# Two-layer hybrid network on one core: the first mixer's order of chunks, delta rule and closing products

## The reference, cut to what matters

```python
def token_mixer(h, w_in, w_out, ...):
    qkv_a, a_a, b_a, z_a, qkv_b, qk_c, v_c, i_c, f_c, o_c = split(h @ w_in)
    qa, ka, va = split(causal_conv_silu(qkv_a, gdn_conv), 3)     # 4 taps, 6 heads of 64
    qa, ka = l2norm(qa), l2norm(ka)
    g = -exp(gdn_a_log) * softplus(a_a + gdn_dt_bias); beta = sigmoid(b_a)
    oa = gated_delta_rule(qa, ka, va, g, beta)   # inverts (I + A), A strictly lower, by blocks
    oa = oa * rsqrt(mean(oa * oa) + eps) * gdn_norm * silu(z_a)
    ob = moba_attention(*split(qkv_b, 3))        # 4 heads, causal here
    qc, kc = split(causal_conv_silu(qk_c, mlstm_conv), 2)
    hc = mlstm_chunkwise(qc, kc, v_c, i_c + i_bias, log_sigmoid(f_c + f_bias))
    hc = hc * sigmoid(o_c); hc = layer_norm_per_head(hc) * mlstm_norm
    return concatenate([oa, ob, hc]) @ w_out
```

## Time and profile before

| | |
|---|---|
| median of 3 runs | 2487.0 us |
| profiled execution | 2486.44 us |
| its span | 2484.6 us |
| mean granted TensorE clock | 0.918 |
| TensorE busy | 2158.2 us (87%) |
| VectorE busy | 1630.8 us (66%) |
| ScalarE busy | 1096.3 us (44%) |
| first mixer stage, first input tile to next stage | 279.4 to 577.4 us |
| second mixer stage | 991.3 to 1289.8 us |

### The profile page before, as it was taken

How to read it: one execution, slowest core, us unless ns; L and a number is a source line. 1 busy time by engine, 2 the same in 40 slices (tenths; PEclk the granted TensorE clock), 3 DMA queues, 4 the chain that set the end, 5 groups by cost and what they waited for, 6 DMA issues and landing times. The chain is left out here.

```text
span 2484.6 us, 35604 instructions
## 1 busy us (share of the span) xinstructions
PE 2158.2 (87%) x14856; PEld 1991.6 (80%) x14856; DVE 1630.8 (66%) x2221; ACT 1096.3 (44%) x1535; POOL 332.8 (13%) x281
## 2 busy tenths in 40 slices
PE   6999887988998999878979986977799979677998
PEld 6998777877997997778969965965699769556996
DVE  6877756448777766664476644874588548746884
ACT  3443452334434444523344433553456346534552
POOL 0000302112001000222030002430110014203000
PEclk9999888988999999889989997987899989887999
DMA  9878431125786665321135642421145534112443
GB/s 379 315 282 314 162 126 60 52 85 203 281 308 238 244 254 212 145 86 60 69 111 221 223 184 93 164 85 52 68 170 187 203 121 153 68 68 72 177 178 117
DMA packets 59792, 409.13 MB, mean 165 GB/s; under 512 B 6832, under 2 KB 7088, under 8 KB 12912
## 3 DMA queue, kind: packets, MB, share of 16 engines
q1 hardware_dynamic: 53424, 384.00, 41.4%
q0 software_dynamic: 5920, 22.43, 2.4%
q10 hardware_dynamic: 288, 0.42, 0.0%
HBM read 403.68 MB, written 3.15 MB: 164 GB/s over the span
## 5 line engine op out<-in xcount | busy, mean ns | idle before, releaser
L573 DVE TENSOR_TENSOR l<-w,h 128x2048 fp32r<-128x2048 f32 x296 | 687.9, 2327 | 251.7 <-ACT h L558 236.2
L674 PE MATMUL ps<-xh,h 128*128 128x256 f32 x2672 | 780.3, 292 | 61.2 <-DVE l L573 29.2
L675 PE MATMUL ps<-xl,h 128*128 128x256 f32 x2672 | 766.7, 287 | 0.0
L676 PE MATMUL ps<-xh,l 128*128 128x256 f32 x2672 | 765.4, 286 | 0.0
L558 ACT CAST h<-w 128x2048 fp32r<-128x2048 f32 x296 | 557.2, 1887 | 314.7 <-PE ps L704 170.7
L674 PEld LDWEIGHTS ps<-xh,h 128*128 128x128 f32 x2672 | 524.4, 196 | 79.9 <-DVE l L573 30.0
L675 PEld LDWEIGHTS ps<-xl,h 128*128 128x128 f32 x2672 | 523.8, 196 | 1.9 <-issue 1.9
L676 PEld LDWEIGHTS ps<-xh,l 128*128 128x128 f32 x2672 | 523.0, 196 | 0.0
L702 PE MATMUL ps<-h,hh 128*128 128x512 f32 x528 | 207.8, 394 | 0.0
L703 PE MATMUL ps<-l,hh 128*128 128x512 f32 x528 | 205.8, 390 | 0.0
L704 PE MATMUL ps<-h,hl 128*128 128x512 f32 x528 | 205.8, 390 | 0.0
(11 more groups left out here) (412 smaller groups left out, 3130.0 us busy)
## 6 DMA issues: line engine op xcount, KB each, us to landing
w<-in_stream SPq DMA_DIRECT2D x362, 1024.0 KB, 4.8
GB<-in_vec POOLq DMA_DIRECT2D x20, 512.0 KB, 6.2
gate<-in_vec POOLq DMA_DIRECT2D x6, 512.0 KB, 4.0
w<-in_stream SPq DMA_DIRECT2D x4, 512.0 KB, 3.7
cst<-in_cst POOLq DMA_DIRECT2D x1, 1160.0 KB, 13.8
memf<-in_memT SPq DMA_DIRECT2D x1, 1024.0 KB, 8.6
xf<-in_xT POOLq DMA_DIRECT2D x1, 1024.0 KB, 10.2
kv<-mk POOLq DMA_DIRECT2D x2, 512.0 KB, 6.9
```

The lines of the kernel that those rows point to most:

```text
L573: e.tensor_tensor(k.L[m % NH][:, 0:z], k.W[n % NW][:, 0:z], k.H[m % NH][:, 0:z], SUB).then_inc(k.lo_done, 1)
L674: p.matmul(P[:, 0:T], H[:, r, o], xh[:, r, :], start=r == 0, stop=False)
L675: p.matmul(P[:, 0:T], H[:, r, o], xl[:, r, :], start=False, stop=False)
L676: i = p.matmul(P[:, 0:T], L[:, r, o], xh[:, r, :], start=False, stop=r == 7)
```

## The change

The 24 gate columns become one chunk of 128 columns in four groups of 6 with 26 zero columns behind each, so that one feature tile has the gates on partitions 0, 32, 64 and 96: `gt`, its copies and its transposes go. The rows' arithmetic reads that tile's bank, which is free again once ScalarE's exponential has read it. The chunks come in another order, `AFTER` is written anew, the delta rule starts with the decays, takes logarithms three together and exponentials three together, uses banks 2, 3, 4, 5 up to the end of the levels, and lets the Q products alternate with the turns; U and V of a level stand behind different tiles. Bank 3 gets a handshake with the adaptive matmuls. The SiLU calls move. The output chunks come in reverse, so that the delta rule's features are needed last, and its last steps stand between and behind output chunks.

```diff
-    tm = [r(1152, 1164) + r(3468, 3480)]
+    row = lambda *at: sum([r(a, a + 6) + [None] * 26 for a in at], [])
+    tm = [row(1152, 3474, 1158, 3468)]
...
-MIX1 = [0, 1, 2, 3, 8, 9, 10, 14, 4, 5, 6, 7, 15, 16, 11, 12, 13]
+MIX1 = [0, 1, 9, 2, 10, 3, 14, 8, 6, 15, 7, 16, 5, 11, 4, 12, 13]
-WOUT1 = [0, 1, 2, 3]
+WOUT1 = [3, 2, 1, 0]
...
 def pe_ada(k, p, m):
+        if 3 in k.freed:
+            p.wait_ge(*k.freed.pop(3))
...
+        k.freed[3] = (k.ada_fin, FIN[v, h] + 1)
...
-GBANK = bank_table((2, 4, 5), nm=3, dk=6, be=2, A=6, Q=6, U0=4, ...)
+GBANK = bank_table((2, 3, 4, 5), dk=6, nm=3, be=2, A=6, Q1=2, U0a=2, Q2=2, U0b=2, Q3=2, ...)
...
+GBANK.update(bank_table((4, 5), u1=1, r2=1, u2=1, o=2, mx=3))
...
-AFTER = ["", "r", "r", "r", "r", "r", "r", "r", "rg", "gg", "gg", "gg", "gg", "gg", "ggb", "ggb", "ggb", "ggb", "ggb", "ggb", "ggb", "ggb", "ggb", "gg", "ggm",
-         "ggm", "ggm", "ggm", "ggm", "gm", "gm", "g", "gmg"]
+AFTER = ["r", "r", "r", "r", "rr", "r", "r", "g", "g", "gg", "", "gg", "g", "gb", "ggb", "ggb", "ggb", "ggb", "ggb", "ggb", "ggb", "ggb",
+         "ggm", "ggm", "ggm", "ggm", "ggm", "ggm", "ggm", "gggm", "gm", "gm"]
...
-    out += [(x,) for x in "gmgmgbm"] + [("out", 0), ("m",), ("m",), ("out", 1)]
+    out += [(x,) for x in "gbmgmgm"] + [("out", 0), ("g",), ("out", 1), ("g",), ("g",)]
...
 def pe_rows(k, p, l):
-    P = take(k, p, 4)
-    p.wait_ge(k.m1_gate, 8 * l + 8)
-    for a in range(2):
-        i = p.transpose(P[:, a * 128:a * 128 + 128], k.gt[:, a, :], k.ident)
...
 def dve_rows(k, v, l):
+    t = TILE[FIRST["win", l, 0]]
+    P, hb = k.ps[t % 2], k.HD[:, 2 * l:2 * l + 1]
     v.wait_ge(*k.rg(l, "zero", 2))
-    v.wait_ge(*k.rp(l, "tr"))
+    v.wait_ge(k.tile_pe, t + 1)
...
 def pe_gdn(k, p, l):
+    yield from pe_decays(...)
     yield
     for i in range(3):        # sums of squares
...
-    yield from pe_decays(...)
...
+    score(0); yield; turn(0); yield; score(1); yield; turn(1); yield; score(2); yield
+    for lv in range(1, 7):    # levels, U0 now being turn()
...
-    p.wait_ge(k.m1_silu, 5 * l + 3)
+    p.wait_ge(k.m1_silu, 5 * l + 5)
...
 def act_gdn(k, e, l):
+    yield from act_decays(...)
     e.wait_ge(*k.lg(STAGES.index(("mix1", l, 0)) - 1, "x", 3))
...
         e.activation(x, rr(bank("nm", i)[:, :], ...), ACT.Ln, bias=1e-6)
-        e.wait_ge(*ga(l, "nm", 2 * i))
+        if i < 2:
+            yield
+    for i in range(3):
+        e.wait_ge(*ga(l, "nm", i))
         e.activation(x, x, ACT.Exp, scale=-0.5)
...
 def act_mix1(k, e, s, feed):
-        if (n, j) == (8, 0):
+        if (n, j) == (3, 1):
             silu(k.gq[:, 0:3, :], 5)
             silu(k.gq[:, 3:6, :], 5)
-        if (n, j) == (15, 0):
-            silu(k.gq[:, 6:9, :], 13)
-            silu(k.cq[:, 0:3, :], 13)
-            silu(k.cq[:, 3:6, :], 13)
+        if (n, j) == (5, 1):
+            silu(k.cq[:, 0:3, :], 9)
+            silu(k.cq[:, 3:6, :], 9)
+        if (n, j) == (12, 0):
+            silu(k.gq[:, 6:9, :], 7)
+        if (n, j) == (12, 1):
+            e.activation(k.zs[:, :, :], k.zs[:, :, :], ACT.Silu)
         if (n, j) == (13, 1):
-            e.activation(k.zs[:, :, :], k.zs[:, :, :], ACT.Silu)
             e.activation(k.so[:, :, :], k.so[:, :, :], ACT.Sigmoid)
...
 def pool_mix1(k, g, s):
-    pool_rms(k, g, l, k.gv, k.gg, ...)
     pool_rms(k, g, l, k.mv_, k.mg, ...)
+    pool_rms(k, g, l, k.gv, k.gg, ...)
```

More of the change, by code:

```diff
@@ L142, in pack @@
         elif k == "win":
-            w = km(inp["w_in"][c[1]][:, MIXCOLS[c[2]][1]])
+            cols = MIXCOLS[c[2]][1]
+            w = np.zeros((D, len(cols)), np.float32)
+            at = [i for i, x in enumerate(cols) if x is not None]
+            w[:, at] = inp["w_in"][c[1]][:, [cols[i] for i in at]]
+            w = km(w)
         elif k == "wout":
@@ L235 @@
     FIRST.setdefault(_c, _n)
-CONVS = [g for n in MIX1 if MIXCOLS[n][0] == "fm" for g in ((2 * n - 2, 2 * n - 1) if n < 10 else (18,)) if g < 15]
+CONVS = [g for n in MIX1 if n and MIXCOLS[n][0] == "fm" for g in ((2 * n - 2, 2 * n - 1) if n < 10 else (18,)) if g < 15]
 def chunk_of(s):
@@ L248, in n_tiles @@
         return 0
-    return 1 if c[0] == "win" and c[2] == 10 else 2
+    return 1 if c[0] == "win" and c[2] in (0, 10) else 2
 TILE = [0]
@@ L1604, in pe_gdn, with score, turn @@
     p.wait_ge(*gv(l, "kb", 2))
[L1605 to L1612, removed]
+    for g in range(6):
+        b = GBANK["A", g]
+        pe_units(k, p, kk, k.kb, g, take(k, p, b)).then_inc(s, 1)
+        k.freed[b] = gv(l, "A", g)
+        if g % 2:
+            yield
+    def score(n):
+        for g in (2 * n, 2 * n + 1):
+            b = GBANK["Q", g]
+            pe_units(k, p, kk, q, g, take(k, p, b)).then_inc(s, 1)
+            k.freed[b] = gv(l, f"Q{n}", g % 2)
+    def turn(n):
+        for g in (2 * n, 2 * n + 1):
+            b = GBANK["U0", g]
+            P = take(k, p, b)
+            p.wait_ge(*gg(l, "part0", g))
+            for j in range(3):
+                i = p.matmul(P[:, j * 128:j * 128 + 128], k.Al[:, 3 * g + j, :], k.ident, start=True, stop=True)
+            i.then_inc(s, 1)
+            k.freed[b] = X0(2 * g)
+    X0 = lambda i: gv(l, "X0" + "ab"[i // 4], i % 4)
+    score(0)
+    yield
+    turn(0)
+    yield
+    score(1)
+    yield
+    turn(1)
+    yield
+    score(2)
+    yield
+    for lv in range(1, 7):
         for g in range(4):
@@ L1699, in dve_gdn @@
     bank = lambda name, i: k.ps[GBANK[name, i]]
+    v.wait_ge(*k.lg(STAGES.index(("mix1", l, 0)) - 1, "x", 3))
+    yield from dve_decays(k, v, l, 0, lambda g: GBANK["dk", g], gp, gv, k.Dk)
     yield
-    for i in range(3):
-        v.wait_ge(*ga(l, "nm", 2 * i + 1))
-        for j in (2 * i, 2 * i + 1):
-            v.scalar_tensor_tensor(out=gq[:, j, :], in0=gq[:, j, :], scalar=0.125 if j < 3 else 1.0, in1=k.rs[:, j, :], op0=MUL, op1=MUL).then_inc(s, 1)
-        yield
-    yield from dve_decays(k, v, l, 0, lambda g: GBANK["dk", g], gp, gv, k.Dk)
+    yield
+    yield
+    for j in range(6):
+        v.wait_ge(*ga(l, "nm", 3 + j // 2))
+        v.scalar_tensor_tensor(out=gq[:, j, :], in0=gq[:, j, :], scalar=0.125 if j < 3 else 1.0, in1=k.rs[:, j, :], op0=MUL, op1=MUL).then_inc(s, 1)
+    yield
     for i in range(3):
```

132 lines of the change are left out of this document (68 added, 64 removed).

## The result

The changed kernel takes 2423.7 us (median of four runs, 2416.9 to 2426.4) against 2486.5 (four runs) for the kernel before: a ratio of 0.9744, 95% interval 0.9717 to 0.9771. It is 62.8 us faster where 42 were forecast. The profiled run took 2425.8 us, 1.8 more than its span. The change is where it was expected: each mixer stage is 31 us shorter, and what lies ahead of, between and behind the two stages changed by +1.4, +0.9 and -1.0 us. The result lies only 2 us above the bottom of the stated range, which was set for rival B.

What follows compares the result with a forecast made beforehand. TensorE, busy 87% of the span, was taken as the bound. Per stage -11.2 + 3 - 10.4 - 4.5 + 1.5 = -21.6, taken as -21; two stages, -42 from 2487, gave 2445 us, range 2422 to 2478.

Steps and rivals of the forecast that it cites:

- rival B: Both mixer stages: clock rises within the first tile and stays, tail gains 6; some 31 us a stage, 2425; chance 0.17.
- Gates as one tile: Stage start: third tile starts 2 us earlier, not 6, as TensorE waits about 3.8 us for the exponential.
- Order of the chunks, Decays first: Up to the first products: fewer evacuation waits, earlier decays, 15 tiles done instead of 13; 11.2 us gained a stage.
- The 3 us taken off for half clock: Ahead of the first products: estimated 3 us a stage lost to half clock after waits near 288 and 335.
- Four banks, scores and turns alternating: First products to end of levels: 10.4 us of waits gained a stage, plus 4.5 from the clock.
- Bank 3's handshake: Adaptive matmuls between levels: TensorE waits at worst 0.5 us for VectorE's addition, elsewhere 0.
- At no cost: Throughout the stage: SiLU calls move with their chunks and GpSimd's norms change places with VectorE's, costing nothing.
- Closing products last: Stage tail: 5.4 us wait behind the sigmoid, 12.8 us of later waits; 1.5 lost, bounds 6 lost to 6 gained.
- A: Only the levels gain, larger waits eat the part before the first products; 13 us a stage, 2461; chance 0.20.
- C: Ninth to nineteenth tile: ScalarE's order is the bound, making the kernel slower; 2505 in all; chance 0.05.
- D: Whole stage: TensorE's waits only move, since the delta rule's VectorE chain takes the time; 2480 to 2487; chance 0.09.
- E: Levels: with four banks a third runs at the lower clock, 28 us more a stage, about 2500; chance 0.03.

Runs made afterwards that it cites:

- The two runs on the tail: Changed kernel plus nine idle matmuls in each mixer stage, 2414.4 us; changed kernel with the tail's sigmoid-dependent mLSTM step one tile later, 2415.8 us.
- the one with the gate path: Changed kernel with GpSimd zeroing the gate buffers first and VectorE taking the gate rows ahead of the low half: 2421.0 us, ratio 0.9734.

## Why the prediction was right in direction and too small

The gain was forecast in the right places and at two thirds of its size. Below are the first stage's 31.1 us by the prediction's own steps. The three stretches are compared at equal work; what was done in another stretch is moved with the durations that the prediction used.

- *Gates as one tile.* As written: no gain that reaches the end. The wait was 4.9, not 3.8, and the run with token tiles shows no difference.
- *Order of the chunks, Decays first.* The chain of rows and the first products were placed within 0.5 us: forecast 309.2 and 353.3, measured 311.1 and 354.9 in a stage that starts 1.4 later, with 15 tiles done. (The start itself lies anywhere from 269.3 to 272.2 in the runs above, counted at the first residual transpose, so the 1.4 is not the change.) That is 1.1 us of length and 9.85 of work ahead (9.15 of tiles, 0.7 of a score), 11.0 of the 11.2 forecast. **The 3 us taken off for half clock were not lost.** Half clock did follow the waits, from 294.6 to 298.0 and from 339.0 to 345.8, but the first products came 74.1 us after the first tile, where the walk had 73.9. Whether the walk already held that half clock or was 3 us too long elsewhere is not shown. The prediction's own sign, first products after about 74 us, left no room for the 3. Of the reasons given for this part, undone alone, the loads are worth about 12 us in the whole kernel, the decays' place some 6 and the chunks some 4. That they add up to twice 11.0 is partly chance, since the chunks' loss lay behind the first products.
- *Four banks, scores and turns alternating.* **This is the term that was mis-sized.** Between the first products and the last tile 24.2 us went (37.0 of length, less the 9.85 above and 2.9 of the solve now done in the tail), where 14.9 were forecast. Waits: 18.3 to 4.7, 13.6 gained for 10.4. Clock and the small rest: 10.6 for 4.5. I expected a third to a half of the waits to stay and to keep their half clock with them. In fact the stretch ran at 1.00 for the 125 us shown above. The run with the bank alone shows that the bank does most of this (clock 0.90 to 0.97, 16.5 us behind the first products), and the run with the scores together shows that the alternation, which the step named beside it, does nothing that can be measured. The step's third reason was never undone alone: in the kernel before, half of a U and half of a V stand between two tiles, in the changed one all of U behind one tile and all of V behind the next. With three banks in both, the waits of V for Xb are 9.7 us in the old slots and 1.9 in the new ones; the order of the chunks differs too, but the slots may well carry a part.
- *Bank 3's handshake* and *At no cost.* One wait of 0.6 for L632 where 0.5 was the bound; none for a SiLU.
- *Closing products last.* The wait behind the sigmoid was forecast at 5.4 and is 5.0. The step's error is in "a little more half clock: 1.5 lost". At equal work the tail is 4.1 us longer (53.6 to 60.6, less 2.9), although TensorE idles less in it (16.4 us, 17.8 before): all of 493 to 512 runs at 0.50, and the output products and the solve take twice their time. GpSimd's powers, of which one took 3.5 before, took 1.4 each. The loss lies within the bound of 6. The two runs on the tail agree: one gives the clock back and leaves VectorE's chain where it was, the other moves the work ahead of the wait, and they gain 9 and 8 us in the whole kernel.

11.0 + 24.2 - 4.1 = 31.1, against 8.2 + 14.9 - 1.5 = 21.6. Rival B had the amount, 31 a stage, with a right reason for part of it (the clock stays up, though only from the levels on) and a wrong one for the rest (the tail gaining). Rivals A, C and D fell with the waits. E, the clock going back and forth with four banks, is refuted by the stretch at 1.00.

What stays open: undone one at a time the parts give about 32 (bank), 12 (loads), 6 and 4 (decays' place and chunks, neither clear of the noise), 0 and 0 us, 54 of 63, and the tail's order loses some 8 in both stages, so that some 17 belong to none of the edits undone. The levels' slots and the closing order as a whole were not undone, and the pairs other than bank and rest were not run. Either the slots carry those 17, or a part undone is caught in part by the others' slack; neither is shown.

## What to carry to other kernels

Price a wait on TensorE with what comes after it: here the half clock behind waits was worth about as much as the waits, on both sides of the account, and useful work placed ahead of a wait instead of behind it gained 6.7 and 4.6 us in the two stages although the wait only moved. An extra bank can pay more than a cleverer order; test the two as a square, since they may simply add. And count table loads in the trace before trusting which functions share a table: with six loads in place of two TensorE had a 6.2 us wait.

## What was not expected of the hardware

- After the 5.0 us wait of the tail the granted clock was 0.50 (the 1.2 GHz level) for some 20 us, although TensorE was busy 16.8 of the 19.5 us from 493.0. With 4.5 us of idle matmuls in that wait it stayed at 1.00. A wait of 1.8 us before a turn at 378 cost no clock at all.
- VectorE's 128x1024 tensor_scalar took 2.89 us beside GpSimd's additions and 0.78 otherwise, the fused add 3.24 and 1.28. GpSimd's three 128x128 copies took 4.30 us beside VectorE's low half, tensor_scalar and fused add and 0.75 without them (first and second line below, the changed kernel and the one with the gate path). The Trainium skill, "SBUF — State Buffer", section "Who interferes with whom", says that a VectorE instruction with two SBUF inputs contends with a GpSimd instruction that reads SBUF. The fused add (inputs `w` and `acc`) and the low half (`w` and `h`) are such instructions, and the trace agrees for them. The tensor_scalar has one tensor input, so that this sentence does not cover its 2.89 us.

```profile
286.23 4.30 POOL L1486 COPY PSEL<-cst 128x128 f32<-128x128 f32 x3
```

```profile
287.37 0.75 POOL L1488 COPY PSEL<-cst 128x128 f32<-128x128 f32 x3
```
